# A decoder layer with a 32-expert MoE on one core: expert weight slots released in halves, residual placed in PSUM by ScalarE, router in token rows, mask by replaced maxima

## What is computed

```
x = x + memory_cross_attention(...)      # ends with o @ w_o, 1024 x 1024
h = rms_norm(x, ffn_norm)
logits = h @ w_router + b_router         # 256 x 32
top_logits, top_idx = top_k(logits, 4)
gates = softmax(top_logits)
for every expert e that a token chose:
    gu = h_rows @ w_gate_up[e] + b_gate_up[e]          # 1024 -> 2048
    gate, up = min(gu[:1024], 7), clip(gu[1024:], -7, 7)
    act = (up + 1) * gate * sigmoid(1.702 * gate)
    out[token] += g * (act @ w_down[e] + b_down[e])    # 1024 -> 1024
result = rms_norm(x + out, final_norm)
```

## Time and profile before

| | |
|---|---|
| median of 3 runs (lowest, highest) | 1266.81 us (1266.59, 1268.41) |
| span of the profiled execution, the only time given for it | 1266.9 us |
| PE busy (matmuls) | 1174.8 us, 93% |
| DVE, ACT busy | 391.4 us, 265.2 us |
| moved by DMA | 454.28 MB, mean 359 GB/s |
| shares of the chain that ended last | PE 52%, DMA 43%, DVE 3% |

### The profile page before, as it was taken

One profiled execution on the slowest core, in us unless ns is written; L12 is line 12 of the kernel. 1 busy time (PEld: TensorE's weight loads), 2 busy tenths in 40 slices (PEclk: granted clock), 3 DMA queues, 4 the chain that ended last, 5 costly groups with the idle time before them and its releaser, 6 DMA issues.

```text
span 1266.9 us, 15355 instructions
## 1 busy us (share of the span) xinstructions
PE 1174.8 (93%) x6173; PEld 619.3 (49%) x6173; DVE 391.4 (31%) x710; ACT 265.2 (21%) x412; POOL 7.5 (1%) x27
## 2 busy tenths in 40 slices
PE   7999999999999999998898999899999889999986
PEld 6998887888633433333333333333433333343422
DVE  5887666546311211111111112112111111121112
ACT  6555445445210101011000011001101100110102
POOL 1000000000000000000000000000000000000000
PEclk9999999999999999999999999989999999999998
DMA  9453323478799999999999999999999999999994
GB/s 325 162 200 136 130 82 121 163 299 313 294 407 427 429 428 427 428 429 429 426 428 429 430 427 427 429 428 428 426 429 430 429 426 414 405 428 429 430 426 186
DMA packets 55078, 454.28 MB, mean 359 GB/s; under 512 B 6332, under 2 KB 6500, under 8 KB 30468
## 3 DMA queue, kind: packets, MB, share of 16 engines
q1 hardware_dynamic: 54864, 453.74, 86.5%
q10 hardware_dynamic: 180, 0.07, 0.0%
HBM read 452.74 MB, written 1.05 MB: 358 GB/s over the span
## 4 chain that ended last, share of the span: by engine, by line
PE 52%; DMA 43%; DVE 3%; issue 1%; DVEq 1%; ACT 1%; SPq 0%; ACTq 0%
DMA ring<-in_moe_w_down 41%; PE ps L874 12%; PE ps L903 12%; PE ps L551 3%; PE ps L553 3%; PE ps L552 3%; PE ps L850 2%; PE ps L566 2%; PE ps L913 2%; PE ps L568 2%; PE ps L567 2%; PE ps L685 1%; DMA wring<-in_ssd_w_in 1%; PE ps L885 1%; DVE wlo L1347 1%
## 5 line engine op out<-in xcount | busy, mean ns | idle before, releaser
L903 PE MATMUL ps<-ring,wring 128*64 128x512 f32 x1024 | 232.5, 600 | 57.5 <-DMA ring<-in_moe_w_down 56.5
L874 PE MATMUL ps<-ring,wring 128*64 128x512 f32 x1024 | 223.3, 594 | 0.0
L903 PEld LDWEIGHTS ps<-ring,wring 128*64 128x64 f32 x1024 | 70.3, 137 | 207.3 <-issue 123.0
L989 ACT ACTIVATE wring<-ps 128x512 f32<-128x512 f32 (+1 forms) x103 | 52.7, 527 | 501.1 <-PE ps L874 431.6
L1675 DVE COPY wring<-ps 128x512 f32<-128x512 f32 x32 | 22.1, 691 | 405.7 <-PE ps L874 405.7
L874 PEld LDWEIGHTS ps<-ring,wring 128*64 128x64 f32 x1024 | 72.1, 137 | 139.7 <-issue 139.6
L1683 DVE TENSOR_TENSOR wring<-ps,bguT 128x512 f32<-128x512 f32 x64 | 41.2, 686 | 310.8 <-PE ps L885 310.8
L874 PE MATMUL ps<-mid,wring 128*64 128x512 f32 x512 | 115.1, 602 | 1.0 <-DVE wring L1683 1.0
L989 ACT ACTIVATE ysb<-ps 128x512 f32<-128x512 f32 x36 | 21.5, 598 | 275.5 <-PE ps L903 269.8
L874 PEld LDWEIGHTS ps<-mid,wring 128*64 128x64 f32 x512 | 35.9, 138 | 69.0 <-issue 68.8
L850 PEld LDWEIGHTS ps<-wring 128*128 128x128 f32 x480 | 55.8, 191 | 23.5 <-issue 23.5
(11 more groups left out here) (314 smaller groups left out, 1388.5 us busy)
## 6 DMA issues: line engine op xcount, KB each, us to landing
ring<-in_moe_w_gate_up SPq DMA_DIRECT2D x64, 2048.0 KB, 23.1
ring<-in_moe_w_down SPq DMA_DIRECT2D x64, 2048.0 KB, 25.5
mid<-in_moe_w_gate_up SPq DMA_DIRECT2D x32, 2048.0 KB, 23.5
wring<-in_moe_w_gate_up SPq DMA_DIRECT2D x16, 2048.0 KB, 26.4
hs<-in_moe_w_gate_up SPq DMA_DIRECT2D x16, 2048.0 KB, 27.9
wring<-in_ssd_w_in SPq DMA_DIRECT2D x10, 2048.0 KB, 8.0
wring<-in_xa_w_kv SPq DMA_DIRECT2D x4, 2048.0 KB, 8.4
wring<-in_ssd_w_out SPq DMA_DIRECT2D x4, 2048.0 KB, 7.7
```

The costliest lines, as they stand in the source:

```text
L874: last = mm(ps[a][SLOTS * half:SLOTS * (half + 1), :], xs[:, m, c % 2, :], w[:, kk, c0:c0 + 512], start=s + kk == 0, stop=s + kk == GP)
L903: last = mm(ps[D_BANK][SLOTS * half:SLOTS * (half + 1), :], act[:, k, :], w[:, kk, 512 * half:512 * (half + 1)], start=k == 0, stop=k == K ...
L989: return nc.scalar.activation(out_, in_, func, **kw)
```

## The change

It does five things.

1. Four of the first expert loads are cut into halves (rows of the slot), each with a wait of its own: down slot 0 of expert 0, and slots 5, 6 and 7 of expert 1. `W_O + 1` now runs over the contraction in two halves with both token blocks in each, the attention output `xo` is laid out in two halves, and `prT` moves to `wring`. New semaphore `wo_half`.
2. The reload of slot 0 with expert 2 is cut in three: a quarter after each half of the first row's matmuls (`gu_part`), then the other row.
3. The residual is put into banks 4 to 7 by four ACT copies (`sum_in`), not by PE (L822 goes).
4. The router multiplies in token rows: `xr` is the stationary operand, 8 matmuls of 32 columns for each token block, straight to bank 0; `lgT`, its copy and L817 go.
5. The mask: the four largest logits are replaced by -3e38 (`match_replace`), and a comparison with the logits marks them; the indices, the cast, the large comparison and the sum go. And the second half of the first gather moves between the second and third slot of the first `gate_up`.

```diff
-        xo = part(hi_ring, 6144, 8192, r=x3, k=KD), part(hi_ring, 4096, 6144, r=x3, k=KD)
+        xo = [(part(hi_ring, c0, c0 + 1024, r=x3, k=4), part(hi_ring, c0 + 1024, c0 + 2048, r=x3, k=4))
+              for c0 in (4096, 6144)]
...
-        prT = part(mid, 4096, 6144, r="p (h c s) -> p h c s", h=XH, c=2)
+        prT = part(wring, WP, WP + 2048, r="p (h c s) -> p h c s", h=XH, c=2)
...
+        def load_gate_up_row(sp, e, odd, s, kk):
+            n = GP * odd + s
+            sp.dma_start(gu_w(n)[:, kk:kk + 1, :], gu_dram[e, s, :, kk:kk + 1, :]).then_inc(g_ready[n], 16)
+
+        def load_down_rows(sp, e, s, half):
+            rows = slice(2 * half, 2 * half + 2)
+            sp.dma_start(dn_w(s)[:, rows, :], dn_dram[e, s, :, rows, :]).then_inc(d_ready[s], 16)
...
             load_gate_up(sp, 1, 1, 0)
+            sp.wait_ge(wo_half, 1)
+            load_down_rows(sp, 0, 0, 0)
             sp.wait_ge(wo_ps, 8)
-            load_down(sp, 0, 0)
+            load_down_rows(sp, 0, 0, 1)
+            sp.wait_ge(wo_half, 2)
+            load_gate_up_row(sp, 1, 1, 1, 0)
+            load_gate_up_row(sp, 1, 1, 2, 0)
             sp.wait_ge(wo_ps, 10)
-            load_gate_up(sp, 1, 1, 1)
-            load_gate_up(sp, 1, 1, 2)
-            sp.wait_ge(hot_ok, 1)
+            load_gate_up_row(sp, 1, 1, 1, 1)
+            load_gate_up_row(sp, 1, 1, 2, 1)
+            sp.wait_ge(normed, 2 * 3 + TC)
+            load_gate_up_row(sp, 1, 1, 3, 1)
             sp.wait_ge(sums_ok, 1)
-            load_gate_up(sp, 1, 1, 3)
+            load_gate_up_row(sp, 1, 1, 3, 0)
+            for a in range(2):
+                sp.wait_ge(gu_part, a + 1)
+                sp.dma_start(gu_w(0)[:, 0:1, 1024 * a:1024 * (a + 1)],
+                             gu_dram[2, 0, :, 0:1, 1024 * a:1024 * (a + 1)]).then_inc(g_ready[0], 16)
+            sp.wait_ge(gu_used, 1)
+            load_gate_up_row(sp, 2, 0, 0, 1)
             sp.dma_start(bdn[0:NE, :], b_down).then_inc(ld_bdn, 16)
...
-            for t in range(TC):
-                split_tokens(W_O + 1, t, 6 + t, xo).then_inc(wo_ps, 1)
+            for half in range(2):
+                for t in range(TC):
+                    last = split_tokens(W_O + 1, t, 6 + t, xo[half], k0=-4 * half, ks=range(4 * half, 4 * half + 4))
+                    if half:
+                        last.then_inc(wo_ps, 1)
+                if half == 0:
+                    last.then_inc(wo_half, 1)
...
-            for half in range(2):
-                pe.wait_ge((hT_act, hT_dve)[half], 2)
-                for j in range(4):
-                    last = mm(ps[0][NE * j:NE * (j + 1), 0:SEQ], wrt[:, 4 * half + j, :], xr[:, 4 * half + j, :],
-                              start=half == 0, stop=half == 1)
-            last.then_inc(rt_ps, 1)
-            pe.wait_ge(lgT_ok, 1)
             for t in range(TC):
-                last = mm(ps[2][:, NE * t:NE * (t + 1)], lgT[:, P * t:P * (t + 1)], sel[:, :], start=True, stop=True)
-            last.then_inc(lg_ps, 1)
-
-            for t in range(TC):
-                for n in range(2):
-                    last = mm(ps[4 + 2 * n + t][:, :], ident, h[:, t, 512 * n:512 * (n + 1)], start=True, stop=True)
-            last.then_inc(sums_ok, 1)
+                pe.wait_ge(hT_act, t + 1)
+                pe.wait_ge(hT_dve, t + 1)
+                for k in range(KD):
+                    last = mm(ps[0][:, NE * t:NE * (t + 1)], xr[:, k, P * t:P * (t + 1)], wrt[:, k, :],
+                              start=k == 0, stop=k == KD - 1)
+                last.then_inc(lg_ps, 1)
+            pe.wait_ge(sums_ok, 1)
...
                 for s in range(GP):
+                    if first and s == 2:
+                        first_gather(1)
...
+                            if first and s + kk == 0:
+                                last.then_inc(gu_part, 1)
...
+            def sum_in(n, t):
+
+                return fn(ps[4 + 2 * n + t][:, :], h[:, t, 512 * n:512 * (n + 1)], ACT.Copy)
...
+            v.memset(mx8[:, :, TOPK:8], 3e38)
+            dve.drain()
             for t in range(TC):
-                v.max_index(ix8[:, t, :], mx8[:, t, :], lg[:, t, :])
-            dve.drain()
-            v.tensor_copy(ix4f[:, :, :].rearrange("p n t -> p t n"), ix8[:, :, 0:TOPK])
-            dve.drain()
-            v.tensor_tensor(eq.rearrange("p (m e) -> p m e", e=NE),
...
-            v.tensor_reduce(mask[:, :, :].rearrange("p t e -> p (t e)"), eq.rearrange("p (n x) -> p x n", n=TOPK),
-                            AX_X, ALU.add).then_inc(mask_ok, 1)
+                v.match_replace(rest[:, t, :], mx8[:, t, :], lg[:, t, :], -3e38)
+            dve.drain()
+            v.tensor_tensor(mask[:, :, :], rest, lg[:, :, :], ALU.not_equal).then_inc(mask_ok, 1)
```

More of the change, by code:

```diff
@@ L193, in build @@
         rank = sb("rank", [P, TC, NCOL + 4])
+        rest = rank[:, :, NE:2 * NE]
         acx = rank[:, :, 0:P]
@@ L238, in build @@
         dtT_ps, dtT_sb = sem("dtT_ps"), sem("dtT_sb")
[L239 to L240 removed]
+        wo_half, gu_part = sem("wo_half"), sem("gu_part")
+        hT_ps, hT_act, hT_dve, wrt_ok, lg_ps, mask4_ok, first_ps, lim_ok = (
+            sem(n) for n in ("hT_ps", "hT_act", "hT_dve", "wrt_ok", "lg_ps", "mask4_ok", "first_ps",
                              "lim_ok"))
@@ L798, in _ @@
                 for t in range(TC):
-                    last = split_tokens(W_O, t, 4 + t, xo, ks=range(4 * half, 4 * half + 4))
+                    last = split_tokens(W_O, t, 4 + t, xo[half], k0=-4 * half, ks=range(4 * half, 4 * half + 4))
                     if half:
                         last.then_inc(wo_ps, 1)
-            for t in range(TC):
-                split_tokens(W_O + 1, t, 6 + t, xo).then_inc(wo_ps, 1)
+                if half == 0:
[5 more added lines that the diff above has]
+                        last.then_inc(wo_ps, 1)
+                if half == 0:
+                    last.then_inc(wo_half, 1)
             ffn_transposes(0)
@@ L829, in _, with first_gather @@
             G_BANK, D_BANK = 3, 2
-            def first_gather():
-                for half in range(2):
-                    for m in range(4):
-                        k = 4 * (m // 2) + 2 * half + m % 2
-                        for t in range(TC):
-                            last = mm(ps[(D_BANK, G_BANK)[half]][:, P * m:P * (m + 1)], xn[:, t, P * k:P * (k + 1)],
-                                      onehot[:, t, :, :], start=t == 0, stop=t == TC - 1)
-                    last.then_inc((first_ps, gath_b)[half], 1)
+            def first_gather(half):
+                for m in range(4):
+                    k = 4 * (m // 2) + 2 * half + m % 2
+                    for t in range(TC):
+                        last = mm(ps[(D_BANK, G_BANK)[half]][:, P * m:P * (m + 1)], xn[:, t, P * k:P * (k + 1)],
+                                  onehot[:, t, :, :], start=t == 0, stop=t == TC - 1)
+                last.then_inc((first_ps, gath_b)[half], 1)
             def gather_half(i, pair, half):
@@ L859, in scatter_transpose, with gate_up @@
                 last.then_inc(st_ps, 1)
-            def gate_up(i, c):
+            def gate_up(i, c, first=False):
                 for s in range(GP):
+                    if first and s == 2:
+                        first_gather(1)
                     if s % 2 == 0:
@@ L955, in _ @@
             pe.wait_ge(normed, 2 * 3 + TC)
-            first_gather()
-            gate_up(0, 0)
+            first_gather(0)
+            gate_up(0, 0, True)
             transposes(0, 0)
@@ L1246, in _ @@
             hT_out(1)
-            act_.wait_ge(rt_ps, 1)
-            fn(lgT, ps[0][:, 0:SEQ], ACT.Copy).then_inc(lgT_ok, 1)
+            sum_in(1, 1).then_inc(sums_ok, 1)
             act_.wait_ge(lmax, 1)
```

45 lines of the change are left out of this document (22 added, 23 removed).

## The result

| | before | after |
|---|---|---|
| median (lowest, highest; 8 runs each) | 1267.6 (1266.31, 1269.6) | 1271.92 (1270.2, 1274.62) |
| ratio, 95% interval | | 1.003 [1.0019, 1.0041] |
| span of the profiled execution | 1266.9 | 1268.6 |
| mean granted PE clock over the runs (before: its 79 runs beside the experiments) | 0.992 | 0.988 |

The change makes the kernel slower by 0.3%, some 3.8 us. The forecast was 1268.5, no change that can be told, with a range up to 1270.1: the median lies above it. The mean clock points at a cause before any trace is opened: 0.0045 less of 1268 us is what 11 us more at 1.2 GHz would give.

What follows compares the result with a forecast made beforehand. The prediction took the weight stream to bound the expert stage, its gapless start set by PE. From 1266.9, 0.4 us won gave 1266.5; 2.1 for the clock gave 1268.6, less 0.1: 1268.5, range 1265.4 to 1270.1.

Steps and rivals of the forecast that it cites:

- The bound: Expert stage: bound by the weight stream, so the kernel's end moves one for one with the moment the stream becomes gapless.
- The hole: DMA stream before the expert stage: idle gap mostly moved, to between 344 and 347, not filled; PE again sets the start.
- The rival of the kept head start: Prefetches in halves: the full 5.6 us head start is kept, giving 1261.3; chance 0.03.
- The structural terms: PE's path from projection to first gate and up, without the clock: its end comes at 361.2, 1.8 us later.
- The reorder: Last projection: the add for token block 0 waits for 36 matmuls instead of 24, moving from 326.46 to 329.2.
- the price of the clock: PE clock falling between 331.9 and 341.85: 1.70 for gate and up plus 0.4 for rank and gather, 2.1 us.
- the like case: Clock fall at the list of extra slots in the earlier trace: gate and up took 15.58 instead of 13.88, 1.70 more.
- The rival of the early fall: Clock falls while the router still runs and comes back late: two stretches slow, 3.4 us, giving 1269.9; chance 0.18.
- the base: Starting time of the sum: 1266.9, the profiled execution of before, taken as 0.1 above the median.
- The split loads: Expert 2's first reload: two added parts each cost an empty start of 1.7, F 2.2 later, 1269.1; chance 0.03.
- the forecast of 0.4 us won without the clock: Start of the gapless stream: F moves from 370.4 to 370.0 at full clock, 0.4 us faster, 1266.5.
- The router rule: PE clock around the router: falls only through idleness, so small matmuls keep it up; sum stays 1266.5; chance 0.25.

Runs made afterwards that it cites:

- e10: Kernel before plus half loads, the reload in three parts and the new mask, with the old projection order, router, residual and gather; ratio 1.0009, median 1269.4 us.
- e7: Kernel before plus half loads, the reload in three parts and the reordered projection; router, residual, mask and gather as before; ratio 1.0012, median 1269.5 us.
- e11: As e10, but ACT fills banks 4 and 5 with the residual and PE fills 6 and 7; ratio 0.9993, median 1267.9 us.
- e13: Kernel before with whole loads, the new mask, and one of four residual copies on ACT, three on PE; ratio 0.9988, median 1266.1 us.

## Why the prediction was wrong

- **The bound held.** The stream behind the first stage is rigid. Span, less the mark, less the loss, is 945.2 before, 944.0 after, and within 1 us of 945.3 in the other runs but one (947.3 in the kernel with the shared residual). So at most about 1 us of the delay is made up over 900 us.
- **The hole was moved, not filled, as said.** Behind the mark it lies at 35.4 to 39.4; the forecast, counted from before's mark, had 33.9 to 36.9 (344 to 347). The start of the gapless stream is set by PE through the release of slots. The rival of the kept head start was rightly put at 0.03.
- **The structural terms held.** The end of the first gate and up was to be 1.8 us later at full clock. It is 54.4 - 49.3 = 5.1 later; of that, the low clock is about 0.7 in the router (4.53 for 3.84; 3.73 in the run with whole loads), 0.7 in the ranks (1.5 for 0.8), and 1.9 in the half gather (3.78 for 1.92), 3.3 in all. That leaves 1.8. The mask was to be ready 1.85 after the router's end and was at 1.86. The reorder was to cost 1.1 and measured 0.8. ACT's copies were to cost nothing, and do.
- **The failed step is the price of the clock: "Price: 1.70 for gate and up, as in the like case, and 0.4 for the parts of rank and gather that also run slowly; 2.1."** That it falls was right. The first fall came at 335.5, in the router, and the gate and up of expert 0 were spared; it cost 3.3. A second fall, at 366, which no part of the forecast had, cost 1.6 more, since the first quarter of gate and up of expert 1 stands ahead of expert 3's first load (load less end is 8.7 after, 7.1 before). Together 4.9, so 2.8 above the price taken: the gapless stream begins 1.7 + 2.8 = 4.5 later, and the loss shows 4.4. I had bounded the price by twice 1.70 for a single fall. The rival of the early fall (1269.9, chance 0.18) named the right moment and was the nearest case, but not the second fall. These prices are worked out from one profile, stretch by stretch: no profile of the changed kernel or of its variants kept the clock at 1.00, so what it would take then is not shown.
- **A second, smaller error: the base.** I added to 1266.9, a span, as if it were a time; the time of that run is 1.8 us above it, 1268.7. The median of eight runs is 1267.6. The sum by its own steps, 1268.6, with 0.7 for the base and 2.8 for the clock gives 1272.1; measured 1271.92. That it comes so close is partly luck: of the fourteen profiles only this one has the second fall, and the runs of after spread over 4.4 us.
- **The split loads** were a rival with 0.03 at 2.2 us. Where the queue sets the start the stream loses 0.7 to 1.4 us more than before with them, at full clock (e10, e7). In the profile of after, PE sets it: the queue had run dry when expert 3's first load came. The mechanism was right and the chance too low. It does not explain this profile, but the forecast of 0.4 us won without the clock had no room for it, and with the clock at 1.00 the changed kernel might show it; no run tells.
- **The router rule.** The Trainium skill, TensorE: Matmul & The Clock Gate, Part 1, says that the clock falls by idleness and comes back by sustained work. The second half agrees with this trace: the clock is back at 345.7, behind 3.78 us of half a gather at the low level. The first half alone would have kept 1.00 through the router; this trace shows 0.87 and then 0.50 while PE's records fill 2.00 of 2.00 us. I weighed row against rule and rightly went by the row, and the earlier trace rows, where 32-row and one-column matmuls had done the same.
- **Two readings were off, without effect.** Before slice 13 the stream moves from a fifth to nearly all of 427 GB/s (82 to 407), not a third to two thirds. And the earlier trace rows leave 3.89 us between a down load's landing and the next wait, not 3.68, which is PE's part of it.

Open: why the clock falls in the router in one run and behind it in another, why it falls a second time at 366, and whether it does so in every run (the mean clock over the runs of after, 0.986 to 0.990, fits both).

## What to carry to other kernels

Before taking PE work away because its result can be had elsewhere, look at what it covers: here, in the kernel before, 3.68 us of wide matmuls stood in front of the critical gather; without them the clock was low in it and it took 2.4 us longer, while they had held the path up by some tenths. Putting such work back behind a router that already runs at the low clock did not help. Price a fall of the clock by every stretch on the path that may run slow until it recovers, and allow for a second one. Compare traces from a mark behind the noise of the earlier stages, and add the sum to the median of the time, never to a span.

## What the hardware showed

- **The clock falls with PE busy.** In after it goes to 0.50 inside 32-column float32 matmuls, 32 records in 4.53 us without a gap, and in two other profiles (e11, e13) just behind the first of the 512-column ones. It does not do so every time: the same 32-column matmuls took 3.73 us at full clock in the run with whole loads. In after it stays low for 10.2 us (335.5 to 345.7); with 5.96 us of matmuls behind the fall it is 7.
- **The first stage has two lengths.** Here is a window of the kernel after, all engines, which answers to the second line of the earlier trace rows:

```profile
266.00:267.00 1.00, 1.00 (x10) 1.00 (x10) 0.83 (x3) 1.00 (x2) 0.00 (x0) 1.00 1.12 475
```

  After the same empty spell the clock is 1.00 here and 0.50 in the profile of before. The fourteen profiles fall apart by this window: in the five with 1.00 the mark lies at 308.3 to 308.8, in the nine with 0.50 at 309.8 to 310.5, whatever the kernel. That is 1.5 us by chance.
- **A copy of 128 x 512 from SBUF into PSUM on ACT costs what one out of PSUM costs**, 0.58 to 0.60 us both ways in after, and four of them fit into ACT's idle time.
- **Loads into a nearly empty queue** start slowly. Parts of 0.5 and 1 MiB one at a time move 242 to 254 GB/s for four microseconds (e10), a whole load of 2 MiB 252 GB/s for two (before), against 428 for queued ones of 2 MiB.
